# Joined falls and a copied likeness in the convolution, late modulations folded by VectorE beside the z gate, and query and key projections in seven products

## The reference

```python
mod = silu(c) @ w_ada + b_ada                     # six vectors of 1024: shift, scale, gain, twice
h = rmsnorm(x, g) * (1 + scale) + shift           # hc the same, from 256 context tokens
q, k, v, z, xbc, dt, gates = split(h @ w_in)
o_na = neighbourhood_attention(rope(q), rope(k), v, kc, vc)
xbc = silu(depthwise_conv(xbc))                   # 5 taps over tokens; 3072 channels -> xs, B, C
Lm[l, s] = exp(a_cs[l] - a_cs[s]) where s <= l    # per head; the same mirrored, backwards
y = (C B^T * Lm) (xs dt) + states ...             # chunks of 128 tokens, 4 groups of 8 heads
y = group_rmsnorm(y * silu(z))
mix = (sigmoid(g_na) * (o_na @ w_na) + sigmoid(g_ssd) * (y @ w_ssd)) @ w_out
```

## Time and profile before

| | us |
|---|---|
| median of 3 runs (3356.49 to 3363.72) | 3363.57 |
| the profiled execution's own time | 3363.13 |
| its span, first to last instruction | 3361.3 |
| PE busy in the span | 2984.4 (89%) |
| DVE busy | 1257.9 (37%) |
| ACT busy | 557.5 (17%) |
| POOL busy | 461.4 (14%) |

### The profile page before, as it was taken

The page is one execution under the profiler, slowest core; times in us unless marked ns, Lnnn a source line. Parts: engine busy times, 40 slices in busy tenths (PEclk is TensorE's granted clock), DMA queues, the critical chain, the costliest instruction groups (busy, mean ns, idle before and its releaser), DMA issues. The chain is left out here.

```text
span 3361.3 us, 38535 instructions
## 1 busy us (share of the span) xinstructions
PE 2984.4 (89%) x15902; PEld 1684.8 (50%) x15902; DVE 1257.9 (37%) x2477; ACT 557.5 (17%) x1091; POOL 461.4 (14%) x326
## 2 busy tenths in 40 slices
PE   6997999988999998989999999987978789996995
PEld 5444775555545776534443443434437753544332
DVE  2235844688645444101101101114365553513113
ACT  2001711455012001000000000002023212301111
POOL 0005030254722330000000000001002200002001
PEclk9998999999999998999999999998989899997998
DMA  7722021342312124699999999995110130054996
GB/s 261 257 92 73 2 80 53 123 155 97 113 63 100 50 101 201 272 429 427 428 428 427 427 428 428 428 427 213 38 38 3 36 109 26 26 225 160 425 424 266
DMA packets 141429, 702.30 MB, mean 209 GB/s; under 512 B 18667, under 2 KB 46990, under 8 KB 108233
## 3 DMA queue, kind: packets, MB, share of 16 engines
q1 hardware_dynamic: 124601, 663.80, 49.3%
q10 hardware_dynamic: 11616, 27.92, 2.2%
q0 software_dynamic: 5040, 8.13, 0.7%
HBM read 697.32 MB, written 22.68 MB: 214 GB/s over the span
## 5 line engine op out<-in xcount | busy, mean ns | idle before, releaser
L2353 PE MATMUL ec_wide<-ec_ring,ec_xg 128*64 128x512 f32 x2048 | 456.2, 600 | 19.7 <-issue 15.5
L2353 PEld LDWEIGHTS ec_wide<-ec_ring,ec_xg 128*64 128x64 f32 x2048 | 147.2, 138 | 308.4 <-issue 304.2
L2387 PE MATMUL ec_acc<-ec_ring,ec_hidT 128*64 128x512 f32 x1024 | 232.0, 608 | 30.7 <-DMA ec_ring<-in_w_exp_down 29.9
L2512 DVE TENSOR_SCALAR ec_xg<-ec_piece,ordered 128x128 f32<-128x128 f32 x64 | 21.9, 405 | 567.5 <-PE ec_piece L2401 567.5
L2387 PEld LDWEIGHTS ec_acc<-ec_ring,ec_hidT 128*64 128x64 f32 x1024 | 81.6, 140 | 178.2 <-issue 178.0
L622 POOL TENSOR_TENSOR rkv_sums<-h2mT 128x1024 f32<-128x1024 f32 x2 | 7.0, 3522 | 1000.4 <-DMA uT<-in_x 1000.4
L2401 PEld LDWEIGHTS ec_piece<-ec_sel,x 128*128 128x128 f32 x512 | 122.9, 336 | 8.6 <-issue 5.7
L2401 PE MATMUL ec_piece<-ec_sel,x 128*128 128x128 f32 x512 | 124.4, 406 | 2.8 <-DVE ec_sel L2494 2.8
L4053 PE MATMUL hm_gu<-hm_ring,hm_xg 128*64 128x512 f32 x432 | 115.9, 605 | 5.4 <-DMA hm_ring<-in_moe_w_gu 2.8
L2476 ACT ACTIVATE ec_hidT<-ec_acc 128x512 f32<-128x512 f32 x32 | 17.4, 594 | 518.8 <-PE ec_acc L2376 518.8
L1445 PE MATMUL conv_main<-hT,conv_early 128*128 128x512 f32 x192 | 86.2, 604 | 2.9 <-DVE bcT L1555 2.9
(11 more groups left out here) (795 smaller groups left out, 5392.2 us busy)
## 6 DMA issues: line engine op xcount, KB each, us to landing
ec_ring<-in_w_exp_gate SPq DMA_DIRECT2D x64, 2048.0 KB, 18.0
ec_ring<-in_w_exp_up SPq DMA_DIRECT2D x64, 2048.0 KB, 27.0
ec_ring<-in_w_exp_down SPq DMA_DIRECT2D x64, 2048.0 KB, 19.6
hm_ring<-in_moe_w_gu SPq DMA_DIRECT2D x27, 2048.0 KB, 25.5
hm_ring<-in_moe_w_down SPq DMA_DIRECT2D x11, 2048.0 KB, 28.2
ahead_qkv<-in_w_in SPq DMA_DIRECT2D x10, 2048.0 KB, 9.6
hm_ring_late<-in_moe_w_down SPq DMA_DIRECT2D x5, 2048.0 KB, 24.8
u2T<-in_moe_w_gu SPq DMA_DIRECT2D x5, 2048.0 KB, 22.9
```

Source lines behind the costliest of these rows:

```text
L2353: last = pe.matmul(wide[half(e), b, :], xg[:, u % 2, j, half(e)], w[e][:, a, b * 512:(b + 1) * 512], start=(j == 0), stop=(j == KD - 1))
L2387: last = pe.matmul(acc[half(e), h, :], hidT[:, f, half(e)], w[e][:, r, h * 512:(h + 1) * 512], start=(f == 0), stop=(f == FT - 1))
L2512: last = dve.tensor_scalar(xg[:, u % 2, j, :], piece[:, m % 2, i * P:(i + 1) * P], scale_cols[:, j:j + 1], shift_cols[:, j:j + 1], ALU.mul ...
```

## The change

Five things are done.

1. **p_q and p_k become `halved_project`** with a `Rope`. DVE shuffles each finished block and multiplies it by the sine (`sign`), POOL multiplies the block by the cosine and adds the two. The eight blocks of a projection are finished at the counts in `complete`.
2. **The late modulations move from p_q to z.** Chunks of `w_ada` are loaded by halves of 1 MB on SP, ahead of z's own later weight loads. DVE folds a half by four chained operations over [128, 512] per piece; PE adds up the partitions by four products with a block of ones for each chunk. `order_columns` moves from p_k to ssd_br_g.
3. **In conv** the cumulative rows are stored negated. ACT's back falls come first in its tile, and DVE joins both falls in one operation per head (`falls`), after it has waited for ACT; it is now DVE that counts up `fallen`. The likeness is copied out of PSUM by ACT (`take_alike`) and masked by POOL. `share_back` of tile i stands in tile i, behind `falls`. `MIX_FIRST` is 6.
4. **PE in conv** waits for ACT's copy of the likeness where it waited for DVE's masks.
5. **In the gated branches** the input sums of the second projection are made by POOL in the first one's stage (`prepare`), so the second has none to make.

```diff
-def halved_project(k, label, w, kt, width, n_chunks, x, sums, extra, out, by_tokens, ahead, then=None, also=None, squash=False, merge=None):
+def halved_project(k, label, w, kt, width, n_chunks, x, sums, extra, out, by_tokens, ahead, then=None, also=None, squash=False, merge=None, rope=None, prepared=False, prepare=None):
...
+            complete = ((1, 0, 0, 0), (2, 0, 0, 1), (7, 1, 1, 0), (9, 1, 1, 1), (11, 0, 1, 0), (12, 0, 1, 1), (13, 1, 0, 0), (14, 1, 0, 1))
...
-            X.make(pool, made)
+            if not prepared:
+                X.make(pool, made)
+            if prepare is not None:
+                prepare.make(pool, made, 4)
+                pool.wait_ge(made, 8)
+            if rope is not None:
...
+                for b in range(8 * units):
...
+                    pool.wait_ge(shuffled, per * (b + 1))
+                    link(pool.tensor_tensor(block, block, k.const(rope.cos)[:, tokens].unsqueeze(1).to_broadcast([P, per, 256]), ALU.mult))
+                    pool.wait_ge(signed, b + 1)
+                    if rope.to_tiles is None:
+                        pool.tensor_tensor(block, block, other[:, b % 2], ALU.add).then_inc(roped, per)
...
+            def sign(b):
...
+                dve.wait_ge(added, PRODUCTS * u + count)
+                if b >= 2:
+                    dve.wait_ge(roped, per * (b - 1))
+                for n in range(per):
+                    dve.stream_shuffle(other[:, b % 2, n], block[:, n], swap).then_inc(shuffled, 1)
+                dve.wait_ge(shuffled, per * (b + 1))
+                dve.tensor_tensor(other[:, b % 2], other[:, b % 2], k.const(rope.sin)[:, tokens].unsqueeze(1).to_broadcast([P, per, 256]),
+                                  ALU.mult).then_inc(signed, 1)
...
+    def fold(self, dve, link, i):
+        m, b = i // 2, i % 2
+        part = self.partial[m % 2]
+        dve.wait_ge(self.half_loaded[b], 16 * (m + 1))
...
+        for j in range(KD // 2):
+            column = self.c[:, b * KD // 2 + j:b * KD // 2 + j + 1]
...
+                link(dve.scalar_tensor_tensor(part, self.halves[:, b, j, :], column, part, ALU.mult, ALU.add))
...
-        ada_product(pe, self.acc, self.cs, self.wt[m % 2]).then_inc(self.product_ready, 1)
+            pe.wait_ge(self.spread_ready, m)
+        for q in range(4):
+            last = pe.matmul(self.acc[q * 32:(q + 1) * 32, 0:P], self.k.const("ones")[:, 0:32], self.partial[m % 2][:, q * P:(q + 1) * P], start=True, stop=True)
...
-MIX_FIRST = 5
+MIX_FIRST = 6
...
-            def fall_together(u):
-                pool.wait_ge(ahead_fallen, u + 1)
-                pool.wait_ge(back_fallen, u + 1)
-                pool.tensor_tensor(fall[:, u % MIX_ROWS], fall[:, u % MIX_ROWS], back_rows[:, :, :], ALU.subtract).then_inc(fallen, 1)
+            def mask_alike(u):
+                pool.wait_ge(alike_taken, u + 1)
...
             def share_ahead(u):
                 c, g = u // SSD_G, u % SSD_G
-                pool.wait_ge(alike_masked, u + 1)
+                pool.wait_ge(alike_masked, 2 * (u + 1))
                 if u >= 2:
                     pool.wait_ge(mix_stored[u % 2], 16 * (u // 2))
...
+                behind = len(alike_at(i - 1)) < 2
+                if not behind:
+                    for u in alike_at(i - 1):
+                        mix(u)
                 for u in alike_at(i):
+                    mask_alike(u)
                     share_ahead(u)
+                if behind:
+                    for u in alike_at(i - 1):
+                        mix(u)
...
-                        pe.wait_ge(alike_masked, alike_at(i - 1)[-1] + 1)
+                        pe.wait_ge(alike_taken, alike_at(i - 1)[-1] + 1)
...
+                for v in falls_at(i - 1):
+                    decay(v)
+                for v in falls_at(i):
+                    back_falls(v)
                 silu(i)
+                for n_at, v in enumerate(alike_at(i)):
+                    take_alike(i, n_at, v)
+                silu_c(i)
...
-            def ahead_falls(u):
+            def falls(u):
                 c, g = u // SSD_G, u % SSD_G
                 dve.wait_ge(rows_loaded[u % MIX_ROWS], 16 * (u // MIX_ROWS + 1))
+                dve.wait_ge(back_fallen, u + 1)
                 for h in range(HG):
...
+                    ins = dve.scalar_tensor_tensor(fall[:, u % MIX_ROWS, h, :], fall[:, u % MIX_ROWS, h, :], cum[:, c, g * HG + h:g * HG + h + 1],
+                                                   back_rows[:, h, :], ALU.add, ALU.max)
+                ins.then_inc(fallen, 1)
...
                 conv_main(i)
-                for v in alike_at(i - 1):
-                    share_back(v)
-                for n_at, v in enumerate(alike_at(i)):
-                    mask_alike(i, n_at * P, v)
                 conv_side(i)
                 for v in falls_at(i):
                     if v == 0:
                         dve.wait_ge(decays_ready, 1)
-                    ahead_falls(v)
+                    falls(v)
+                for v in alike_at(i):
+                    share_back(v)
...
-            for g in range(2, SSD_G):
-                sp.wait_ge(product_ready, LT * (g - 1))
-                sp.dma_start(ahead.buffer(g % 2, KD, 512), z_cols[:, :, g * 512:(g + 1) * 512]).then_inc(ahead.loaded[g % 2], 16)
+            for i in range(len(pieces)):
+                late.load(sp, i)
+                g = i // LT + 1
+                if i % LT == 2 and 2 <= g < SSD_G:
+                    sp.wait_ge(product_ready, LT * (g - 1))
+                    sp.dma_start(ahead.buffer(g % 2, KD, 512), z_cols[:, :, g * 512:(g + 1) * 512]).then_inc(ahead.loaded[g % 2], 16)
...
+                late.fold(dve, fold_link, i)
...
+                       prepare=HalfSums(inT, feats, sums))
```

More of the change, by code:

```diff
@@ L720, in _ @@
                 product(u, 1, X.x12, w21)
-                pe.wait_ge(made, 2)
+                if not prepared:
+                    pe.wait_ge(made, 2)
                 pe.wait_ge(folded, 4 * u + 3)
@@ L776, in _ @@
                 for i in range(2):
+                    sign(8 * u + 2 + i)
+                for i in range(2):
                     dve.wait_ge(product_ready, done + 11 + i)
@@ L780, in _ @@
                 for i in range(2):
+                    sign(8 * u + 4 + i)
+                for i in range(2):
                     dve.wait_ge(product_ready, done + 13 + i)
@@ L1900, in _ @@
                     take(i - 7)
+                if i >= 4 and i % 2 == 0:
+                    late.take(dve, (i - 4) // 2)
+                if i >= 5 and i % 2:
+                    late.keep(dve, (i - 5) // 2)
+                late.fold(dve, fold_link, i)
             for i in range(len(pieces) - 5, len(pieces)):
@@ L1903, in _ @@
                 take(i - 2)
+                if i == len(pieces) - 5:
+                    late.take(dve, late.steps - 2)
+                if i == len(pieces) - 3:
+                    late.keep(dve, late.steps - 2)
+                    late.take(dve, late.steps - 1)
+                if i == len(pieces) - 1:
+                    late.keep(dve, late.steps - 1)
+                    late.finish(dve, fold_link)
             for i in range(len(pieces) - 2, len(pieces)):
@@ L1908, in z_gate_norm, with gated_branch @@
     ahead.count += 16 * (SSD_G // 2)
[L1911 removed]
+def gated_branch(k, label, w_gate, hT, w, feats, inT, uT, add, ahead, spaces, then=None, from_tiles=False, also=None):
     nc = k.nc
@@ L2094, in first_mixer @@
                                             vc[:, t, bass.ds(c * 512, 512)]) for t in range(CT_TILES)], ahead=ahead, then=(w_q, KD, 512))
[L2095 to L2098 removed]
                     with ExitStack() as s3:
[L2100 removed]
+                        extra = tile(s3, "qkv_extra", [P, KD * 512])
+                        rough = v[:, :, :].rearrange("p t (a n) -> p (t a) n", n=L)
+                        halved_project(k, "p_q", w_q, KD, 512, 2, hT, flat(uT), extra, rough, False, ahead, then=(w_k, KD, 512),
+                                       rope=Rope("na_cos_q", "na_sin_q", rope_loaded, q))
+                        halved_project(k, "p_k", w_k, KD, 512, 2, hT_tiled, flat(uT), extra, key, False, ahead, then=(w_v, KD, 512),
+                                       rope=Rope("na_cos_k", "na_sin_k", rope_loaded))
                         halved_project(k, "p_v", w_v, KD, 512, 2, hT_tiled, flat(uT), extra, v, True, ahead)
```

191 lines of the change are left out of this document (108 added, 83 removed).

## The result

The changed kernel takes 3448.2 us (median of 4 runs, 3447.9 to 3451.7), the kernel before 3363.1 beside it (3356.5 to 3363.7): ratio 1.026, 95% interval 1.025 to 1.028. It is slower, as forecast, but by 85 us and not by 26, and 3448 lies far above the range, which ended at 3408.

A forecast was written before the change was run, and what follows sets the result against it. PE, busy 89% of the span, was taken to bound the kernel. From 3363.1 us: conv +49, p_q and p_k -23.5, z +8.6, gated branches -8.2, giving 3389; range 3363 to 3408.

The forecast's parts named there:

- The closed chain in conv: In conv tiles 10 to 20, falls, store, share_ahead, share_back and taps wait in a ring: 18.2 us a tile against 13.1.
- The two rivals that lived on a shorter landing: In conv: store off the path, 3315 us, 8%; or store landing in about 2.9 us, 3363 us, no change, 10%.
- The third rival, a slow PE: In conv, PE's clock stays at its lower level through idle time: 22.8 us a tile, total 3440, chance 4%.
- `share_back` 2.2: In conv, the link of DVE's share_back in each tile's chain was taken as 2.2 us.
- Tile 10 ... +2: In conv, tile 10 starts 2 us later, at 666 for 664.1; an estimate, 0 to 6.
- z, "+8.6": In z, PE's small products and transposes, the last fold, keep and finish add 8.6 us, 5 to 14; other folds hidden.
- p_q and p_k, "118": p_q 56.8, p_k 59.8 and p_v's cold start 1.4 together take 118 us for 141.5, a gain of 23.5.
- The gated branches, "-8.2": In ssd_br_b, PE's 6.10 us wait and slowed products go as sums are made earlier: -8.2 us, -9 to 0.
- Behind ssd_br_b, "0": From p_out to the end, no change in time was forecast: 0 us.
- The rival "the store stays off the path": In conv, share_ahead finds its buffer stored and DVE's 10.8 us hide under PE's 11.4: total 3315 us, chance 8%.

The follow-up runs named there:

- experiment 1: The changed kernel with MIX_FIRST back at 5, so the joined falls stand a tile earlier: 3381.8 us, ratio 1.006.
- experiment 2: The changed kernel with the store ahead of load_back in SP's list for a unit, MIX_FIRST still 6: 3383.1 us, ratio 1.007.
- experiment 6: The kernel before with MIX_FIRST 6 alone, keeping the old two falls, POOL's subtraction and masks on DVE: 3484.0 us, ratio 1.037.
- Experiment 3: The changed kernel with POOL's mix of the unit before always ahead of the masks and share_ahead: 3424.4 us, ratio 1.020.
- experiment 5: The changed kernel with DVE taking and keeping z's small products ahead of gate(i): 3432.2 us, ratio 1.021.
- experiment 4: The changed kernel with the conv of the kernel before and MIX_FIRST 5: 3363.0 us, ratio 1.0006.
- experiment 8: The changed kernel with the store ahead of load_back on SP and POOL's mix ahead of masks and share_ahead: 3366.2 us, ratio 1.0013.
- experiment 7: The kernel before with only the gated branches' input sums made by POOL one stage earlier: 3349.6 us, ratio 0.9968.

## Why the prediction was wrong in size and right in direction

**The closed chain in conv: right.** The forecast said that with the falls in the tile of their likeness the store would come onto DVE's path, and named each link. Experiments 1, 2 and 6 show it: taking either SP's order or the place away opens it, putting the place alone into the kernel before makes it. The landing of the store, from which the range was made, was 5.41 us in the tile shown, until POOL started, and 5.3 in the median of twelve, the 5.3 of the earlier trace rows. The DMAs of conv from 650 to 880 us (size, median us from issue to landing):

```profile
ssd_mix_rows<-conv_shares SPq DMA_DIRECT2D x12, 512.0 KB, 5.3
conv_back_rows<-ssd_cum_rows SPq DMA_DIRECT2D x11, 512.0 KB, 4.4
y<-ssd_cum_rows SPq DMA_DIRECT2D x10, 512.0 KB, 6.2
```

The two rivals that lived on a shorter landing fall with it. The Trainium skill ("DMA: Bandwidth & Descriptors", anatomy of one DMA) gives its fit for the GpSimd path, and the 3.2 us that I had worked out from it as an estimate were not met by this store, which SP issues within 1 us of two others of its size. In experiment 1, where `load_back` often leaves 2.2 us ahead of it, the store's median from 650 to 820 us was 3.7. The third rival, a slow PE, falls too: the clock did drop (0.84 in the eleven tiles, with side products of 6.44 us where the earlier trace rows has 3.69), and PE's products still fitted in the longer tile.

**The step that failed: "`share_back` 2.2".** The forecast took it from a row where POOL was idle beside it. In the changed kernel POOL's `mix` stands right behind `share_ahead`, so it starts in the same moment as `share_back`. From tile 11 to 20 that took 4.25 to 4.27 us each time; in tile 10, where no `mix` stands beside it, it took 2.19. Ten times 2.1 is 21 of the 28.8 us by which conv was mis-sized. In tile 21 the falls are hit instead (5.45 us). Experiment 3, which moves `mix` alone, brought `share_back` back to 2.19 in all of these tiles. How the two meet is seen in DVE's line over the whole run (duration min, median, max in ns of one operation):

```profile
L1689 DVE SCALAR_TENSOR_TENSOR conv_shares<-y,dt,conv_shares x128: 337/340/2426, 626.0 to 887.3; 128x128 f32<-128x128 f32 x128
```

Most of the 128 operations take 0.34 us; the longest takes 2.43, about one whole `mix` (2.35). So DVE does not run at half speed beside POOL: one of its operations stands until POOL's instruction has ended. The Trainium skill has a rule for this ("SBUF — State Buffer", section on the two separate sides): a DVE operation with two SBUF inputs and a POOL instruction that reads SBUF contend for a shared pair of ports, and whichever starts first holds it for its whole instruction. The trace agrees: `mix` starts at 726.95 and `share_back` at 727.02. The taps, which read one of their tensors from PSUM, were 3.10 us with `mix` beside them and without. The forecast had the same slowing in its rows for p_q and ssd_br_b and did not apply it here.

**"Tile 10 ... +2" (0 to 6): +6.5.** Tile 10 starts 124.2 us behind conv's first main product instead of 117.7. Tiles 8 and 9 hold two units each, and falls, masks and two `share_ahead` meet there: the falls of tile 8 took 6.22 us. No run takes this part to pieces. Tiles 10 to 21: 221.8 us against the 200 forecast. From tile 21 to z it was -1.3 and not -4. Together 4.5 + 21.6 + 2.7 = 28.8.

**z, "+8.6": +26.7.** The count of work was right: DVE is busy 51 us longer (42.97 to 94.11; I had 50), hidden beside PE, and the weights came in time. The step that failed is that I took the eight products and transposes as PE's time alone, 2.4 and 2.2 us, and did not ask who is ahead of DVE's copy between them. DVE's list puts it behind `gate(i)`, which waits for product i and ACT; PE's transpose stands behind that product. Without that wait (experiment 5) z takes 137.4, +10.3, near the forecast; products and transposes themselves took 3.6 and 3.0 us in the changed kernel.

**p_q and p_k, "118": 122.2.** p_k took 60.0 as forecast (59.8), p_q 62.2 for 56.8. The timeline of PE in the changed p_q, the same product in experiment 1 (second line), and POOL in the rope:

```profile
127.07 8.83 PE L741 MATMUL p_q_acc<-uT,qkv_extra 128*128 128x256 f32 x32 [2.25 <-DVE qkv_extra L802]
...
127.48 7.14 PE L741 MATMUL p_q_acc<-uT,qkv_extra 128*128 128x256 f32 x32 [2.24 <-DVE qkv_extra L802]
...
172.97 2.47 PE L741 MATMUL p_k_acc<-hT_tiled,ahead_qkv 128*128 128x256 f32 x5 [9.44 <-PEq L636]
...
157.60 1.27 POOL L700 TENSOR_TENSOR v<-v,const_rope 128x512 f32<-128x512 f32 x1
...
160.65 1.27 POOL L700 TENSOR_TENSOR v<-v,const_rope 128x512 f32<-128x512 f32 x1
...
171.12 1.40 POOL L708 TENSOR_TENSOR q<-v,p_q_other 128x256 f32<-128x256 f32 x2
```

DVE's folds of the weights began only when a load had landed, at 117.64, 6.9 us into the stage, and the second of them took 4.33 us beside POOL's sums. So PE waited 2.25 us for the third, and then ran a slow product (8.83 us for 7.07): 4.0 of the 5.4. The wait stands in the profiles of experiments 1, 4 and 8 too, which change nothing here; the slow product stands in 4 (8.77) and not in 1 and 8 (7.14 and 7.15), where p_q took 60.5. So those 1.7 us differ from one execution to another. The tail of the rope behaves as forecast in kind: POOL needs 3.05 us a block and ends at 172.5, some 9 us behind PE's last product. No run changed the wait or the tail.

**The gated branches, "-8.2": right.** ssd_br_b -8.3 (107.0 to 98.7), its 6.10 us wait gone:

```profile
1230.40 7.07 PE L741 MATMUL ssd_br_b_acc<-xs,y 128*128 128x256 f32 x32
```

**Behind ssd_br_b, "0": +8.2, open.** Nothing there was changed. p_out is 2.1 us longer (59.2 to 61.3) with a clock of 0.95 for 0.98, the rest is spread. The kernels with the rest of the change show +3.6 to +9.7 there, experiments 6 and 7, built on the kernel before, -0.9 and +1.3. So it seems to go with the change, but its size moves by 6 us between executions, and which part causes it was not settled.

**The rival "the store stays off the path".** Its price was wrong. I gave it 3315, with DVE's 10.8 us under PE's 11.4. Experiments 1 and 2 are that case, and they took 3382 and 3383: a tile is 14.2 us of DVE's work as POOL's operations lie there, and 12.5 in experiment 8, the best measured. Even with the chain away the new conv is not 25 us faster: 401.7 us in experiment 8 against 404.5 before.

So of the 59 us missed, 28.8 are conv, 18.1 z, 8.2 the stages behind, and the other 4.2 p_q and p_k (the small terms left cancel).

## What to carry to other kernels

When a step is moved, write down the closed chain that it makes, and then read for each link which engine works beside it in the new order, for a duration that was read beside an idle engine is not its price elsewhere. Work that hides in busy time can still cost a wait: look for the consumer queued in order on the bound engine, and at what stands ahead of the producer on its own. Two orders (the copy ahead of the gate, `mix` beside operations that read PSUM) took an edit of one to four lines and were worth 16 and 24 us (17 with the chain open, 3383.1 to 3366.2).

## What was not expected of the hardware

- Operations of DVE with two SBUF inputs stood still while POOL's instructions ran: 8 of them took 4.20 to 6.31 us for 2.18, by how many POOL instructions they met. POOL is held as well: in the changed kernel a `mix` that began at 628.22, while a `share_back` ran until 630.24, took 4.25 us, and the next one, beside the main taps, 2.36. POOL's L1460 from 626 to 636 us (duration min, median, max in ns):

```profile
L1460 POOL TENSOR_TENSOR conv_shares<-conv_shares,y x2: 2358/3304/4249, 628.2 to 632.4; 128x1024 f32<-128x1024 f32 x2
```

- With the chain open and the contention still there, most tiles take 13.7 or 14.6 us in turn, as `share_back` meets POOL or only the falls do; the mean does not show this.
